# A two-layer hybrid decoder on one core: a merged look-up, a compression input on another engine, batches placed engine by engine, and another end

## What is computed

```python
def _peer(h, wq, sub_keys, u, v):
    q = (hf @ wq).reshape(T, PEER_HEADS, 2, PEER_HALF)
    s_half = jnp.einsum('thpc,pnc->thpn', q, sub_keys)
    v_half, i_half = lax.top_k(s_half, PEER_TOPK)
    cand = (v_half[:, :, 0, :, None] + v_half[:, :, 1, None, :]).reshape(...)
    cand_idx = (i_half[:, :, 0, :, None] * PEER_KEYS + i_half[:, :, 1, None, :]).reshape(...)
    top_s, top_pos = lax.top_k(cand, PEER_TOPK)
    expert_idx = jnp.take_along_axis(cand_idx, top_pos, axis=-1)
    gate = jax.nn.softmax(top_s, axis=-1)
    act = gelu(einsum('cd,chkd->chk', hc, u[ic]))
    out = einsum('chk,chkd->cd', gc * act, v[ic])
```

## Time and profile before

| | us |
|---|---|
| median of 3 runs | 1760.89 (1759.98 to 1761.31) |
| the profiled execution | 1762.63 |
| its span | 1760.8 |
| TensorE busy | 1338.8 (76%) |
| VectorE busy | 1094.5 (62%) |
| GpSimd busy | 663.1 (38%) |
| ScalarE busy | 515.2 (29%) |
| moved by DMA | 689.00 MB, mean 391 GB/s |

### The profile page before, as it was taken

One profiled execution on the slowest core, in us unless ns is written; L12 is line 12 of the kernel. 1 busy time (PEld: TensorE's weight loads), 2 busy tenths in 40 slices (PEclk: granted clock), 3 DMA queues, 4 the chain that ended last, 5 costly groups with the idle time before them and its releaser, 6 DMA issues. The chain is left out here.

```text
span 1760.8 us, 22766 instructions
## 1 busy us (share of the span) xinstructions
PE 1338.8 (76%) x8310; PEld 686.1 (39%) x8310; DVE 1094.5 (62%) x2746; ACT 515.2 (29%) x1295; POOL 663.1 (38%) x1028
## 2 busy tenths in 40 slices
PE   8999886679999857667888766767888865565655
PEld 5856842245564523222354433233354531111111
DVE  5510588984333849779434757798444868964444
ACT  3411232262312222226332222225332323221112
POOL 0000234344333424435434434344433545565451
PEclk9999988799999978878989888778999977887778
DMA  9755599999999999999999999999999999999996
GB/s 387 293 169 182 209 421 421 414 394 422 411 421 421 420 410 405 421 396 414 422 421 422 421 421 420 422 386 421 421 421 421 421 418 400 407 420 422 421 421 272
DMA packets 95728, 689.00 MB, mean 391 GB/s; under 512 B 11008, under 2 KB 11136, under 8 KB 12288
## 3 DMA queue, kind: packets, MB, share of 16 engines
q0 software_dynamic: 73728, 536.90, 74.0%
q1 hardware_dynamic: 21888, 150.64, 21.3%
HBM read 685.40 MB, written 2.10 MB: 390 GB/s over the span
## 5 line engine op out<-in xcount | busy, mean ns | idle before, releaser
L521 POOL DMA_INDIRECT uv_rows<-uv_in,idx x512 | 504.0, 984 | 1055.5 <-PE acc_pe L1307 817.5
L1307 PE MATMUL acc_pe<-uv_rows,diag 64*64 64x512 f32 x4096 | 616.5, 731 | 322.7 <-ACT diag L1036 307.9
L566 DVE CUSTOM_DVE_ANT_0 uv_rows<-uv_rows,h_ps 128x1024 f32<-128x1024 f32 x512 | 606.7, 1218 | 232.4 <-DMA uv_rows<-uv_in,idx 220.6
L1307 PEld LDWEIGHTS acc_pe<-uv_rows,diag 64*64 64x64 f32 x4096 | 154.5, 153 | 693.1 <-ACT diag L1036 481.8
L1029 ACT ACTIVATE gelu_b<-act_b,h_scale 128x2 f32<-128x2 f32 x255 | 75.0, 294 | 744.0 <-DVE act_b L566 739.1
L1337 PEld LDWEIGHTS bank<-h_t,w_own 128*128 128x128 f32 x1504 | 171.0, 193 | 18.0 <-issue 18.0
L1361 PE MATMUL bank<-w_own,h_t 128*128 128x512 f32 x384 | 176.0, 612 | 2.3 <-ACTq L1077 2.2
L1337 PE MATMUL bank<-h_t,w_own 128*128 128x128 f32 x1504 | 175.1, 278 | 0.0
L515 POOL TENSOR_TENSOR diag<-ident_st,gate 128x64 f32<-128x64 f32 x512 | 159.0, 311 | 9.6
L1036 ACT ACTIVATE diag<-diag,gelu_b 128x64 f32<-128x64 f32 x510 | 149.6, 340 | 8.3
L1361 PEld LDWEIGHTS bank<-w_own,h_t 128*128 128x128 f32 x384 | 73.2, 196 | 107.8 <-issue 103.7
(11 more groups left out here) (208 smaller groups left out, 1170.5 us busy)
## 6 DMA issues: line engine op xcount, KB each, us to landing
w_own<-blocks_in SPq DMA_DIRECT2D x112, 1024.0 KB, 10.5
uv_rows<-blocks_in SPq DMA_DIRECT2D x24, 1024.0 KB, 10.4
uv_rows<-uv_in,idx POOLq DMA_INDIRECT x512, 15.4
xs<-x_in SPq DMA_DIRECT2D x2, 512.0 KB, 13.5
uv_rows<-mem_in SPq DMA_DIRECT2D x1, 1024.0 KB, 13.8
mem_gained<-uv_rows SPq DMA_DIRECT2D x1, 1024.0 KB, 14.1
area<-mem_gained SPq DMA_DIRECT2D x1, 1024.0 KB, 8.9
smalls<-smalls_in SPq DMA_DIRECT2D x1, 816.5 KB, 13.5
```

What stands on the lines that cost most here:

```text
L521: nc.gpsimd.indirect_dma_start(uv_rows[:, slot_of(k, earlier), :, :].rearrange("p a n -> p (a n)"), None, a["uv"], bass.IndirectOffsetOnAx ...
L566: v.tensor_tensor_reduce(u_row, u_row, h_ps[:, :], 1.0, 0.0, ALU.mult, ALU.add, act_b[:, k // B % AHEAD, k % B:k % B + 1]).then_inc(sems[" ...
L1307: mm = pe.matmul(acc_pe[c * HT:(c + 1) * HT, r * BLK:(r + 1) * BLK], diag[tok, slot_of(k), :], uv_rows[tok, slot_of(k), 1, c * BLK:(c + 1) ...
```

## The change

Five things are edited.

1. `look_up` handles high and low bits together. The first part makes both positions (a shift, a mask, one conversion), scales the high half's indices by 128 and adds the base, and compares with 0 to 15 over 1024 elements for two heads. The second part is a multiplication over 1024, a sum of 32 at a time, which gives high x 128 + base + low at once, and a conversion to `idx`.
2. `cmp_inputs` leaves VectorE and becomes a step of ScalarE: eight copies without the position code, and one that puts the codes into the 16th column. The product is linear, so TensorE's result for that column is what the codes add; `ident_kind` gets ones in the 16th row of each group, by which the turning matmul adds it to the other 15.
3. The table of batches is not worked out from lengths but written out, for each step as (VectorE, ScalarE, TensorE), one table a stage.
4. At the end, TensorE puts the residual into `acc_pe` at the start of the last stage and adds the experts on top, laid out by token; ScalarE squares `acc_pe` itself, and VectorE scales it, so the four additions fall away. ScalarE takes a dummy root behind its last diagonal, which brings the root's table.
5. The filler matmuls are gone.

```diff
-                  ("w2", 256), ("pe", 64), ...
+                  ("w2", 256), ("pe", 32), ...
...
-TURNS = spread(PLAN, NB - 2)
-MEM_TURNS = spread(MEM_PLAN, NB - 2)
-LAST_TURNS = spread(LAST_PLAN, 21)
+BATCHES = {
+    1: {
+        "start": (1, 0, 0), "mix_norm": (0, 2, 1), "rank_more1": (0, 0, 1), "ab": (1, 1, 0), "rank_pairs1": (1, 1, 0),
...
+        "gates3": (2, 6, 0), "look_up3": (1, 0, 0), "look_up_more3": (10, 7, 6), "first_out": (34, 35, 40),
...
+ENGINES = ("vector", "scalar", "tensor")
...
-                    n = turns.get(name, {}).get(step_name, 0)
+                    n = batches[step_name][ENGINES.index(name)] if step_name in batches else 0
...
                     def experts_end():
+                        if last:
+                            return
...
+                            of_head = ident_kind[:, :, :].rearrange("p k (v n) -> p (k v) n", v=KV_HEADS)
+                            step.mark(v.tensor_tensor(
+                                of_head[:, :, 0:N_CMP], of_head[:, :, 0:N_CMP],
+                                of_head[:, :, N_CMP:NC].to_broadcast([P, 2 * KV_HEADS, N_CMP]), ALU.add))
...
-                        e, op, by = ((0, ALU.logical_shift_right, 4), (1, ALU.bitwise_and, 15))[part]
-                        step(v.tensor_scalar(top_q, top_p[:, heads[0]:heads[0] + n, :], by, None, op))
-                        step(v.tensor_copy(pos_f, top_q))
...
-                        step(v.tensor_reduce((e_hi, pos_f)[e], one_hot, AX.X, ALU.add))
                         if part == 0:
+                            if heads[0] == 0:
+                                step.mark(v.tensor_copy(expert_base[:, :], small("first")))
+                            where = top_p[:, heads[0]:heads[0] + n, :]
+                            step.mark(v.tensor_scalar(pos_q[:, :, :, 0], where, 4, None, ALU.logical_shift_right))
+                            step(v.tensor_scalar(pos_q[:, :, :, 1], where, 15, None, ALU.bitwise_and))
+                            step.mark(v.tensor_copy(pos_f, pos_q))
+                            step(v.tensor_scalar(half_f[:, :, 0, :], half_f[:, :, 0, :], float(PK), expert_base[:, :],
+                                                 ALU.mult, ALU.add))
+                            shape = [P, n * TOPK * 2, TOPK]
+                            step(v.tensor_tensor(one_hot.rearrange("p (s i) -> p s i", i=TOPK),
...
+                        step(v.tensor_tensor(hot, hot, half_f.rearrange("p h e i -> p h (e i)").unsqueeze(
+                            2).to_broadcast([P, n, TOPK, 2 * TOPK]), ALU.mult))
+                        row = pos_f[:, :, 0:8, :].rearrange("p h k e -> p h (k e)")
+                        step(v.tensor_reduce(row, hot, AX.X, ALU.add))
+                        v.tensor_copy(idx[:, TOPK * heads[0]:TOPK * (heads[0] + n)].rearrange(
+                            "p (h k) -> p h k", h=n), row).then_inc(sems[signal], 1)
...
+                                s.activation(roots[:, 0:1], zero[:, 0:1], ACT.Sqrt)
                                 return
...
+                    def cmp_inputs():
+
+                        for kvh in range(KV_HEADS):
+                            for half in range(2):
+                                for hi in range(2):
...
+                                    s.activation(
+                                        cmp_in[half * HD:(half + 1) * HD, :, hi * 8:hi * 8 + 8,
+                                               kvh * NC:kvh * NC + N_CMP],
+                                        tok.rearrange("p k (n c e) -> p k c n e", c=8, e=2)[:, :, :, :, half],
+                                        ACT.Copy).then_inc(sems["cmp_in_built"], 1)
...
-                            act.wait_ge(sems["experts_added"], 2 * c + 2)
-                            s.activation(junk[:, c * BLK:(c + 1) * BLK], xs[:, D + c * BLK:D + (c + 1) * BLK],
+                            act.wait_ge(sems["sums_done"], c + 1)
+                            s.activation(junk[:, c * BLK:(c + 1) * BLK], acc_pe[:, c * BLK:(c + 1) * BLK],
...
-                            if last and k >= PAIRS - 3 * B and k % B == 0:
-                                for _ in range(3):
-                                    pe.matmul(bank[0][:, :], ident[:, :], mem_v[:, 0, 0:BLK], start=True, stop=True)
...
-                        pe.wait_ge(sems["cmp_in_built"], 16)
+                        pe.wait_ge(sems["cmp_in_built"], 9)
...
+                            for c in range(2):
+                                pe.matmul(acc_pe[:, c * BLK:(c + 1) * BLK], ident[:, :],
+                                          xs[:, D + c * BLK:D + (c + 1) * BLK], start=True, stop=False,
+                                          skip_group_check=True)
```

More of the change, by code:

```diff
@@ L178 @@
-LAG = 1
-AT_START = 1
-def spread(plan, within):
-    lengths = [LENGTH[name if name in LENGTH else name.rstrip("0123456789")] for name in plan]
-    vector, tensor, done, passed = {"start": AT_START}, {}, 0, 0
-    for name, length in zip(plan, lengths):
-        passed += length
-        due = within * passed // sum(lengths)
-        vector[name] = due - done
-        tensor[name] = max(due - LAG, 0) - max(done - LAG, 0)
-        done = due
-    scalar = {**vector, "start": 0, plan[0]: vector[plan[0]] + AT_START}
-    tensor[plan[0]] += AT_START
-    return {"vector": vector, "scalar": scalar, "tensor": tensor}
@@ L331, in stage @@
             plan = LAST_PLAN if last else FIRST_PLAN if first else PLAN if mem_layer is None else MEM_PLAN
-            turns = {} if first else LAST_TURNS if last else TURNS if mem_layer is None else MEM_TURNS
+            batches = {} if first else BATCHES[dense]
             if dense is not None:
@@ L931, in look_up @@
-                        if part == 0:
-                            return
-                        if heads[0] == 0:
-                            step(v.tensor_copy(expert_base[:, :], small("first")))
-                        step(v.tensor_scalar(e_hi, e_hi, float(PK), expert_base[:, :], ALU.mult, ALU.add))
-                        v.tensor_tensor(idx[:, TOPK * heads[0]:TOPK * (heads[0] + n)].rearrange(
-                            "p (h k) -> p h k", h=n), e_hi, pos_f, ALU.add).then_inc(sems[signal], 1)
+                        q, n, h0 = heads[0] // 2, len(heads), heads[0] % 2
@@ L1003, in _ @@
                             cols = slice(c * BLK, (c + 1) * BLK)
-                            rows = xs[:, D + c * BLK:D + (c + 1) * BLK]
-                            v.scalar_tensor_tensor(out=rows, in0=rows, scalar=st[:, 3:4], in1=final_gain[:, cols],
+                            v.scalar_tensor_tensor(out=xs[:, D + c * BLK:D + (c + 1) * BLK], in0=acc_pe[:, cols], scalar=st[:, 3:4], in1=final_gain[:, cols],
                                                    op0=ALU.mult, op1=ALU.mult).then_inc(sems["out_ready"], 1)
```

110 lines of the change are left out of this document (62 added, 48 removed), and 37 rows, old and new, of the table BATCHES.

## The result

| | us |
|---|---|
| before, median of 4 runs | 1761.10 (1759.98 to 1764.14) |
| changed, median of 4 runs | 1777.43 (1774.73 to 1778.90) |
| ratio | 1.0088, 95% interval 1.0071 to 1.0106 |
| span of the changed kernel's profile | 1775.9 |

What follows compares the result with a forecast made beforehand. Bound by DMA bytes of gathered rows and weights. End 4.4 + look-up 0.9 + regained lapses 8.5 = 13.8 us off the profiled 1762.63 gives 1748.8, or 1747.1 us on the runs' scale; range 1738 to 1757.

Steps and rivals of the forecast that it cites:

- What bounds the kernel: From the second stage on, DMA bytes of gathered rows and weights; lapses below 421 GB/s total 18.2 us.
- The end: From last dot to span's end: no fillers, additions or late table load; saves 4.4 us, bounds 2.8 and 4.9.
- The look-up: Before the first gather: fewer, larger passes start it 0.9 us sooner, counting in full; bounds 0.5 and 1.2.
- the quarters: Look-ups for a quarter of two heads: about 0.85 us less VectorE work each, four times a stage.
- The compression input: Sixteen additions, 5.7 us a stage, leave VectorE; ScalarE gets nine copies taking 3.3 us.
- The relief of VectorE: VectorE has 8.2 us less work a stage by the 1150 us lapse; 8.5 us of lapses counted as regained.
- The batches: Engines take batches at different places; five sixths of 10.2 us of lapses with VectorE busy regained, 8.5 us.
- the slower one: Rival: eight long VectorE stretches without a batch starve the queue, 3.7 us each, 29.6 of lapses; 1767.0 us, chance 0.08.
- the compression's stall moves to ScalarE: Rival: copies stand ahead of gelus on ScalarE; 5.5 us at 1140 and 740 not regained; 1752.6 us, chance 0.10.
- that of the slower rival: Sign of being wrong: third stage under 414 GB/s, GpSimd waiting over 20 us for slots in its first 60.
- the signs of a right forecast: End 10.3 us; copies 0.3 to 0.4; compression windows at least 380 GB/s; last-stage exponential wait under 2; stages at least 418.
- the prediction's "nothing" for this edit: Two matmuls bringing the residual into the sums at the last stage's start: no cost, uncovered at most 0.5 us each.

Runs made afterwards that it cites:

- the even layout: Changed kernel with the kernel before's evenly laid-out batches in place of the written-out table in all stages, other edits kept: 1751.5 us, ratio to before 0.9927 to 0.9958.

## Why the prediction was wrong

- **What bounds the kernel**: right. Time followed the lapses below 421 GB/s; the 21.1 us of new ones are the result.
- **The end**: forecast 4.4 us, the trace has 4.5 (14.7 to 10.2). The dummy root came 0.02 us after the table load and the first square 0.11 after that. The Trainium skill (ScalarE: Activation LUTs, What ACT_TABLE_LOAD costs) adds a drain of 1.38 us to a switch; nothing of the kind shows here either, so taking the row and not the page was right. Put back by itself the old end gives a smaller difference past the last dot, 3.5 us, and a larger one by the medians, 7.3, so the match of 4.4 and 4.5 is in part luck.
- **The look-up**: forecast 0.9 us. From the first maximum of the ranking ahead of it to the first gather it was 10.65 us (187.84 to 198.49) and is 9.49 (187.04 to 196.53), 1.2 less. The gather starts 2.0 us sooner in all; the other 0.8 came ahead of the ranking. For the quarters the term was too large: 0.85 us of VectorE was forecast for each, and the groups of the second stage give 21.4 us before and 19.0 after for four, 0.6 each.
- **The compression input**: the term was mis-sized on ScalarE. I took 3.3 us for nine copies from rows of 128 x 256; they took 4.8, eight of 0.60 that overlap to 4.51 and one of 0.31. On VectorE the sixteen additions are gone, as forecast.
- **The relief of VectorE**: the regain of 8.5 us was too much even where the table does no harm. With the even layout the four stages lose 3.9, 3.8, 0.9 and 3.7 us, 12.3 in all, 5.9 fewer than before.
- **The batches**: here the prediction fell, at the term of 8.5 us regained; measured are 21.1 us lost. "I take five sixths of the 10.2 us as regained" counted the table as a gain because VectorE had less to do, and its price only as stretches of VectorE work without a batch. A slot is held from the gather until TensorE has added its row. I had the table's counts per step for all three engines and looked at VectorE's alone; TensorE falls to five batches behind it, which is every slot there is, and dense steps that the others wait for were put behind batches that wait for a landing. Both can be seen from the order, but the count alone is no price: the engines come to the same step at different times, and in the fourth stage the table has VectorE up to seven ahead (`win_out`: 39 against 32), where 3.7 us are lost, as before. In the lapses followed above, what costs is a step that others wait for, or a batch that would free slots, standing in an engine's order behind something that is not ready, while the slots are full.
- **The rivals**: the slower one had the sign and the effect (the queue runs dry) at 1767.0, with a chance of 0.08, and VectorE's lumps as its cause, which fit the lapse at 824 and not those at 556 and 876. That the compression's stall moves to ScalarE came true at one place, 12.2 us of TensorE's time. Together they deserved far more than 0.18. The top of the range was added up short, 1.4 us for low bounds that come to 2.0 (1.6 and 0.4); it changes nothing.
- **The signs**: that of the slower rival came as it was worded, a third stage at 406 GB/s and GpSimd waiting 27.2 us in its first 60 (until 670.23). But it was badly chosen: that stretch, 644 to 704 us, moves 419 GB/s; during the wait 6.45 of the 9.67 MB moved between 646 and 669 us came by the hardware queue, which carries SyncE's weight loads, and the fastest kernel has the same wait (27.3 us). Here such a wait cost transfers only where the queues had run empty. Of the signs of a right forecast the end came (10.2 us) and VectorE's wait for the gates' exponentials (0.5 us in the last stage); copies of 0.3 to 0.4 us, no window at the compression under 380 GB/s and stages at 418 did not.

What is not settled: what VectorE's and what ScalarE's places each cost (a table with only TensorE near the even layout and the other two in full was not run), whether the table would cost the same on the kernel before, without the other four edits (not run either), and why the even layout on the fourth and last stages is 4 to 6 us better than what I put there.

The fastest version is the changed kernel with its table held within one batch of the even layout in the second and third stages, and the even layout in the fourth and last: 1749.9 us, 0.9931 of the kernel before (0.9912 to 0.9949). The plain even layout at 1751.5 is not told apart from it.

## What to carry to other kernels

When engines with queues of their own share a ring of buffers, write down at each step how many units each has done, for all of them and not for the busiest alone. Where the first user is ahead of the one that frees by the whole ring, look what stands in the freeing engine's order: a step that others wait for must not stand behind one that waits for a transfer. The distance itself is not the price (with seven in the fourth stage 3.7 us were lost, as before), and none at all was worse than two, since the engine then stands before the one ahead. Try a written-out schedule against an even one before believing that freed engine time will be used. And take GB/s, not the wait of the engine that issues, as the sign that a queue runs dry.

## What the runs showed of the hardware

The copies on ScalarE that reorder their elements took longer than plain ones. The groups by line and shape of the changed kernel (count, busy us, mean ns, idle before):

```profile
L1173 ACT ACTIVATE area<-kv_t 64x240 f32<-64x240 f32 x32 | 17.8, 602 | 0.3
```

240 elements in 602 ns, where 256 in a plain order took 372 to 417. The Trainium skill (ScalarE: Activation LUTs, What ACT_TABLE_LOAD costs) gives 186 ns and 0.833 for each element, which makes an estimate of 386 ns here; the measurement decides. Whether it is the pattern or the 64 partitions was not taken apart.

The layout of the sums in the last stage costs TensorE time. The adding of rows in 1560 to 1700 us, with the new layout and then with the old one, both with even batches and the same number of rows:

```profile
L1421 PE MATMUL acc_pe<-uv_rows,diag 64*64 64x512 f32 x454 | 103.7, 595 | 37.0 <-ACT diag L1135 37.0
```

```profile
L1421 PE MATMUL acc_pe<-uv_rows,diag 64*64 64x512 f32 x448 | 81.1, 858 | 58.1 <-ACT diag L1132 58.1
```

By the code a pair's matmuls went to four combinations of input and output half, and now go to two. A matmul lasts 595 ns in place of 858, but fewer run at once: 454 x 595 ns is 2.6 times the busy time, 448 x 858 is 4.7 times. So TensorE is busy 103.7 us in place of 81.1, although the granted clock in this window is 1.00 with the new layout (2.4 GHz throughout) and 0.74 with the old one (in part at 1.2 GHz). TensorE waits less for diagonals with the new layout, 37.0 us against 58.1. It costs nothing here, since both move 421 GB/s, but the prediction's "nothing" for this edit had not counted it.
